# Both FFN matmuls as 2x2 block products with 7 block matmuls instead of 8, weight sums formed on chip, weights streamed once per 1024 tokens

## The chip, the cores and the metric

The kernel runs on all 8 cores of one Trainium2 chip. Each core computes one of the 8 batch elements with the same program and its own copy of the weights in HBM; the cores exchange nothing. The metric is the time on the device, in microseconds, of the slowest core. A core has TensorE (PE, matmuls, with PEld for its weight loads), VectorE (DVE), ScalarE (ACT), GpSimd (POOL) and SyncE (SP), which only issues transfers. POOL issues transfers too, in its own queue, in order with its other instructions.

## The reference

A decoder block on x (2048 tokens by 1024 channels a core). The first part (gated spatial mixing, dilated attention, gates, output projection) is the same in both kernels. The change is in the second part, which is, for each core:

```python
h = rms_norm(x, norm_ffn_pre[l])                       # 2048 x 1024
f = jnp.square(jax.nn.relu(h @ w_ff1[l])) @ w_ff2[l]   # 1024 -> 4096 -> 1024
x = x + rms_norm(f, norm_ffn_post[l])
```

## The kernel before

The program is written as a list of operations with reads, writes and a priority (`P.prio`). A planner (`Plan.schedule`) then plays the list through with a cost for each operation and fixes one static order for each engine's queue; semaphores are put in from the same order. So a change in one place moves instructions in others, and an engine that reaches an instruction whose input isn't there waits, with everything behind it.

The stages in time are: load and norm of x; attention, eight pairs of heads (`hp`), with the value projection for the spatial gating (tiles `hTc`, weights `wva`) mixed into its end; the u projection; gating (`G0`), which for 8 column blocks and 4 token windows runs 32 matmuls each and writes `merged`; output projection for 16 token tiles of 128 (`F0`); FFN (`L0`).

Output projection: for a tile, 16 matmuls into banks 4, 5 or 6, 7; ACT squares them, POOL makes the inverse root, DVE scales (L974), adds x (L976) and scales again (L981), PE transposes the tile and ACT copies it into `h2T`, which shares the memory of `merged`. The first four tiles (`NEARLY`) are done inside the last gating block.

FFN before: four windows `w` of 512 tokens. FFN 1 makes 32 blocks `fb` of 128 hidden channels by 8 matmuls each (128x128 weights, 512 tokens moving), ACT takes relu out of PSUM (L1011), DVE squares (L1012). FFN 2 makes, for each of four token tiles, 2 halves by 32 matmuls; then the norm, the addition of x1 (which was stored to DRAM by the output projection and comes back into `xi[i % 2]`, L1020) and the store of `out` (L1041), both issued by SP. All weights sit in SBUF for the whole FFN: `w1` (8 tiles) and `w2`, bf16. They are f32 in DRAM. Transfers of POOL turn them to bf16 in DRAM during gating (list `conv`, L863 to L869) and load them from there (`load_w1`, `load_w2`), w2 in 16 pieces over the memory of `hT` and `ybT` once FFN 1 has begun.

FFN 1 of window 0 needs only token tiles 0 to 3, so its matmuls stand between those of the output projection of the later tiles.

The softmax here doesn't subtract the row's maximum and nothing guards it: scores larger than these inputs give would overflow.

## Time and profile before

| what | us |
| --- | --- |
| median of 3 runs | 1232.25 (1231.87 to 1414.58) |
| the profiled execution's span | 1230.0 |
| PE busy in it | 1166.0 (95%) |
| DVE busy | 563.4 (46%) |
| ACT busy | 521.4 (42%) |
| DMA engines, share over the FFN | 0.0 to 0.2 |

The span runs from the first to the last instruction of the slowest core and is 2.25 us under the median. Of its stages, attention and everything up to gating end at about 505 us, gating at 725, the output projection at 785, and the last matmul ends at 1222.5. The granted clock of PE is 0.99 of full speed in the mean. The busy shares are of the whole span; what a stage costs is read from its own rows.

### The profile page before, as it was taken

The page shows a single profiled execution, that of the slowest core. Times are in us where ns is not written, and L with a number is a line of the kernel's source. Part 1 is how long each engine was busy: PE and PEld are TensorE (multiplying, and loading weights), DVE is VectorE, ACT ScalarE, POOL GpSimd, SP SyncE. Part 2 cuts the span into 40 slices and gives each one's busy share as a digit, 9 for nine tenths or more (in the row PEclk, how much of TensorE's full clock was granted, in tenths as well). Part 3 has the DMA queues.
Part 4 walks back from the last instruction along what each step waited for, and adds up shares of the span by engine and source line. Part 5 has one row for each costly group of instructions (what it writes and reads, how often), then busy time and mean ns, then how long its engine had stood idle before and what let it go on. Part 6 is the DMA issues. An engine that isn't in the chain of part 4 may idle for free.

```text
span 1230.0 us, 20225 instructions; the slowest of 8 cores (1225.0 to 1230.0 us)
## 1 busy us (share of the span) xinstructions
PE 1166.0 (95%) x7560; PEld 588.8 (48%) x7560; DVE 563.4 (46%) x941; ACT 521.4 (42%) x806; POOL 105.8 (9%) x201
## 2 busy tenths in 40 slices
PE   4799999999898999999999999999999999999997
PEld 2476555665454445444444444444444444444443
DVE  5757777777776346632323357621131122112211
ACT  5437887778765752122121246631132123113311
POOL 0000000001014220000000124410000000000000
PEclk9899999999998999999999999999999999999999
DMA  9464434423313335499968767690200120021011
GB/s 240 126 159 96 115 89 111 106 51 92 80 27 68 63 72 86 84 121 128 128 89 117 120 202 261 226 317 32 76 35 1 65 73 1 3 84 52 1 35 69
DMA packets 59073, 119.91 MB, mean 97 GB/s; under 512 B 36769, under 2 KB 36897, under 8 KB 56482
## 3 DMA queue, kind: packets, MB, share of 16 engines
q0 software_dynamic: 9440, 52.43, 25.7%
q1 hardware_dynamic: 49538, 66.19, 17.5%
q8 instruction: 62, 1.02, 0.3%
q14 instruction: 33, 0.27, 0.1%
HBM read 133.29 MB, written 37.75 MB: 139 GB/s over the span
## 4 chain that ended last, share of the span: by engine, by line
PE 88%; ACT 3%; DVE 3%; issue 3%; DMA 2%; POOL 1%; SPq 0%; ACTq 0%; DVEq 0%; POOLq 0%
PE pst L195 87%; ACT sb_Et L618 2%; DMA sb_xt<-x 1%; PE pst L199 1%; DMA sb_wva<-w_va 1%; DVE sb_xn L489 1%; DVE sb_PT L630 0%; DVE sb_xn L981 0%; POOL sb_st L964 0%; ACT sb_Lr L689 0%; DVE sb_hT L495 0%; ACT sb_junk L966 0%; DVE sb_ybT L694 0%; POOL sb_st L962 0%; ACT sb_gc L798 0%
## 5 line engine op out<-in xcount | busy, mean ns | idle before, releaser
L195 PE MATMUL pst<-sb_w,sb_hid 128*128 128x512 bf16 x1024 | 221.7, 379 | 2.8 <-issue 1.4
L195 PE MATMUL pst<-sb_merged,sb_w 128*128 128x512 bf16 x1024 | 222.8, 379 | 0.0
L618 ACT ACTIVATE sb_Et<-pst 128x1024 bf16<-128x1024 f32 (+1 forms) x160 | 150.4, 973 | 45.5 <-PE pst L195 37.5
L195 PEld LDWEIGHTS pst<-sb_w,sb_hid 128*128 128x128 bf16 x1024 | 100.1, 98 | 124.1 <-issue 3.7
L195 PEld LDWEIGHTS pst<-sb_merged,sb_w 128*128 128x128 bf16 x1024 | 100.1, 98 | 120.1
L1011 ACT ACTIVATE sb_hid<-pst 128x512 bf16<-128x512 f32 x128 | 76.3, 596 | 128.2 <-PE pst L195 127.9
L630 DVE TENSOR_TENSOR sb_PT<-sb_Et,sb_EB 128x1024 bf16<-128x1024 bf16 (+2 forms) x200 | 110.1, 569 | 40.8 <-ACT sb_Et L618 25.6
L195 PE MATMUL pst<-sb_hT,sb_wqk 128*128 128x512 bf16 x512 | 126.4, 394 | 0.9 <-DVE sb_hT L495 0.9
L1012 DVE TENSOR_TENSOR sb_hid<-sb_hid 128x512 bf16<-128x512 bf16 x128 | 54.3, 425 | 142.8 <-ACT sb_hid L1011 141.8
L907 ACT ACTIVATE sb_sg<-pst,sb_small 128x512 f32<-128x512 f32 x64 | 44.0, 687 | 172.7 <-PE pst L195 156.2
L195 PE MATMUL pst<-sb_hT,sb_wg 128*128 128x512 bf16 x512 | 116.7, 379 | 0.0
L1025 ACT ACTIVATE sb_junk<-pst 128x512 bf16<-128x512 f32 x32 | 19.1, 597 | 196.3 <-PE pst L195 196.3
L1028 DVE TENSOR_TENSOR sb_st<-sb_st 128x1 f32<-128x1 f32 x16 | 2.6, 160 | 182.9 <-ACT sb_junk L1025 182.9
L195 PEld LDWEIGHTS pst<-sb_hT,sb_wg 128*128 128x128 bf16 x512 | 49.8, 98 | 58.5
L195 PEld LDWEIGHTS pst<-sb_hT,sb_wqk 128*128 128x128 bf16 x512 | 47.2, 101 | 61.5 <-issue 17.6
L911 DVE SCALAR_TENSOR_TENSOR sb_sg<-sb_sg,pst 128x512 f32<-128x512 f32 x32 | 22.0, 687 | 98.6 <-PE pst L195 98.6
L195 PE MATMUL pst<-sb_wva,sb_hTc 128*128 128x512 bf16 x256 | 61.0, 391 | 4.5 <-DMA sb_wva<-w_va 3.0
L195 PE MATMUL pst<-sb_PT,sb_V 128*128 128x64 bf16 (+3 forms) x1280 | 62.4, 205 | 1.5 <-DVE sb_ybT L694 1.5
L195 PE MATMUL pst<-sb_hT,sb_wu 128*128 128x512 bf16 x256 | 58.9, 387 | 4.7 <-DVE sb_ybT L694 4.1
L195 PE MATMUL pst<-sb_QT,sb_KT 64*128 64x256 bf16 (+1 forms) x768 | 52.7, 250 | 10.7 <-ACT sb_Et L618 10.7
L195 PE MATMUL pst<-sb_ybT,sb_wg 128*128 128x512 bf16 x256 | 60.5, 379 | 1.8 <-DVE sb_tmpm L844 1.8
L195 PE MATMUL pst<-sb_wout,sb_merged 128*128 128x512 bf16 x256 | 58.8, 379 | 1.8 <-DVE sb_xo L972 1.3
(97 smaller groups left out, 1232.7 us busy)
## 6 DMA issues: line engine op xcount, KB each, us to landing
sb_xt<-x SPq DMA_DIRECT2D x16, 512.0 KB, 11.5
sb_xo<-x SPq DMA_DIRECT2D x16, 512.0 KB, 5.8
sb_wg<-w_g POOLq DMA_DIRECT2D x8, 1024.0 KB, 10.8
w_bf<-w POOLq DMA_DIRECT2D x16, 512.0 KB, 10.4
x_scr<-sb_xo SPq DMA_DIRECT2D x16, 512.0 KB, 6.4
sb_xi<-x_scr SPq DMA_DIRECT2D x16, 512.0 KB, 3.7
sb_w<-w_bf POOLq DMA_DIRECT2D x16, 512.0 KB, 17.9
out<-sb_xi SPq DMA_DIRECT2D x16, 512.0 KB, 2.6
```

Of the source, the lines that this page charges most:

```text
L195: e.matmul(out, lhsT=l, rhs=r, start=st, stop=sp, skip_group_check=True))
L199: fns = [lambda e, a=a, b=b: e.transpose(out=a, in_=b, identity=ident) for a, b in outs_ins]
L489: P.dve(lambda e, b=b, n=n, i=i: e.scalar_tensor_tensor(out=xn[n % NXN][:], in0=xt[b][:], scalar=stat[:, 16 + i:17 + i], in1=gbc[:], op0=A ...
L618: P.act(lambda e: e.activation(out=et[:, :, 0:W], in_=psall[:, sb:sb + 2, 0:W], func=AF.Exp, scale=0.125), 2 * W, [], [et.key()], [sb, sb ...
L630: P.dve(lambda e: e.tensor_tensor(out=o, in0=i0, in1=i1, op=ALU.mult), n, rk, [pt.key()], rate=2, name="mask")
L907: P.act(lambda e, j=j, cb=cb, pj=pj, s_=s_: e.activation(out=s_[j][:], in_=pj, func=AF.Tanh, scale=0.5, bias=small[:, bg_c + 8 * j + cb:bg ...
L911: P.dve(lambda e, pj=pj, s_=s_: e.scalar_tensor_tensor(out=s_[1][:], in0=s_[1][:], scalar=1.0, in1=pj, op0=ALU.add, op1=ALU.mult), 512, [s ...
L1011: P.act(lambda e, fb=fb, bk=bk: e.activation(out=hid[:, fb, :], in_=ps(bk), func=AF.Relu), 512, [], [hid.key(fb)], [bk])
L1012: P.dve(lambda e, fb=fb: e.tensor_tensor(out=hid[:, fb, :], in0=hid[:, fb, :], in1=hid[:, fb, :], op=ALU.mult), 512, [hid.key(fb)], [hid.k ...
L1025: P.act(lambda e, hf=hf, bb=bb, s_=s_: e.activation(out=junk4[:, 0:512], in_=ps(bb[hf]), func=AF.Square, accum_out=s_[:, 8 + hf:9 + hf]), ...
L1028: P.dve(lambda e, s_=s_: e.tensor_tensor(out=s_[:, 10:11], in0=s_[:, 8:9], in1=s_[:, 9:10], op=ALU.add), 1, [s_.key((8, 10))], [s_.key((10 ...
```

## The change

FFN 1 and FFN 2 are each written as a product of 2x2 block matrices by 7 block products in place of 8 (sums and differences of blocks of both factors go in, and sums of products come out).

- Weights. Blocks: for FFN 1 the 1024 input channels in 2 halves and the 4096 hidden ones in 2 halves; for FFN 2 the 4096 in 2 and the 1024 in 2. The conversion to bf16 in DRAM is now 32 transfers of POOL, one behind each class of attention (`pv_class`), so that it is done when gating starts. In gating, `prep` (32 times) loads 0.5 MB of four bf16 blocks by SP into a ring `PB`, DVE forms four sums (128x512 each), and SP stores them, 0.5 MB, as `w1_comb` and `w2_comb`.
- Streaming. The FFN runs twice, for `s` = 0, 1, each with 1024 tokens (two windows n1, n2 are the two column blocks). The weights no longer stay in SBUF. A ring of 5 slots takes, by SP, 16 pieces `r1` of 7 blocks (0.92 MB) and 14 pieces `r2` (1.05 MB) in each pass: 58.7 MB in all.
- FFN 1: for each `g` of 16, seven groups (`mmp`) of 4 matmuls into a pair of banks. Between them ACT copies intermediate sums out of PSUM to f32 tiles `sn` (3 a g) and does one relu; DVE adds a PSUM bank and a copy (3 a g, `evict`), does two relus and two squares. DVE forms the token-side sums `TB` and, in place, a quarter of `h2T` ahead of each pass.
- FFN 2: seven block products `o`, each 4 token tiles `p` by 2 halves of hidden channels by 8 matmuls, with DVE forming the sums `S1` and parts of `hid`, copies `s1`, `u2`, `u3` (the same tiles `sn`, 12 in all), and additions `acc`. A token tile is finished (`fin`) behind block product 5 (tiles 4 to 7 of the pass) and 6 (tiles 0 to 3): POOL makes the inverse root; DVE does four operations; the loads of `xi` and the stores of `out` are now issued by POOL. There are still two buffers `xi`.
- Matmuls of both FFN parts: 1792 in place of 2048, each 128x128 by 512 as before.

```diff
+    conv = []
+    for g in range(16):
+        conv.append(lambda g=g: P.dma("pool", lambda e: e.dma_start(out=w1b_d[g], in_=w1_d[g]), 1e6, f"cv{g % 2}", [],
+                                      [P.nkey(("w1b", g))], after=anchor[0]))
+    for h in range(4):
+        for q in range(4):
+            c = slice(2048 * h, 2048 * h + 2048)
+            conv.append(lambda q=q, h=h, c=c: P.dma("pool", lambda e: e.dma_start(out=w2b_d[q][:, c], in_=w2_d[q][:, c]), 1e6, f"cv{q % 2}", [],
...
+            if conv:
+                P.prio = b0 + (11 + 3 * c) * 5 + 1
+                conv.pop(0)()
...
+    def prep(n, prio):
+
+        g = n % 16
+        pb = PB[n % 4 if n < 24 else n % 2]
+        ki, ko = pb.key((0, 4)), pb.key((4, 8))
+        c = f"pb{n % 4 if n < 24 else n % 2}"
+        if n < 16:
+            P.dma("sp", lambda e: e.dma_start(out=pb[:, 0:4, :].rearrange("p q c -> p (q c)"), in_=w1b_d[g]), 0.5e6, c + "l",
+                  [P.nkey(("w1b", g))], [ki], prio=prio)
+        else:
+            P.dma("sp", lambda e: e.dma_start(out=pb[:, 0:4, :], in_=w2b_d.rearrange("q p c -> p q c")[:, :, 512 * g:512 * g + 512]), 0.5e6,
+                  c + "l", [P.nkey(("w2b", q, g // 4)) for q in range(4)], [ki], prio=prio)
+        for o, i0, i1, op in ((4, 0, 3, ALU.add), (5, 4, 1, ALU.subtract), (6, 1, 0, ALU.subtract), (7, 2, 5, ALU.subtract)) if n < 16 else (
+                (4, 0, 1, ALU.subtract), (5, 3, 4, ALU.subtract), (6, 3, 0, ALU.subtract), (7, 2, 5, ALU.subtract)):
+            P.dve(lambda e, o=o, i0=i0, i1=i1, op=op: e.tensor_tensor(out=pb[:, o, :], in0=pb[:, i0, :], in1=pb[:, i1, :], op=op), 512,
+                  [pb.key(i0), pb.key(i1)], [pb.key(o)], prio=prio + 3, rate=2, name="comb")
+        if n < 16:
+            P.dma("sp", lambda e: e.dma_start(out=w1c_d[g], in_=pb[:, 4:8, :].rearrange("p q c -> p (q c)")), 0.5e6, c + "s", [ko],
+                  [P.nkey(("w1c", g))], prio=prio + 4)
+        else:
+            P.dma("sp", lambda e: e.dma_start(out=w2c_d.rearrange("q p c -> p q c")[:, :, 512 * g:512 * g + 512], in_=pb[:, 4:8, :]), 0.5e6,
+                  c + "s", [ko], [P.nkey(("w2c", g))], prio=prio + 4)
     rot = [0]
...
-        if 2 <= cb < 4:
-            load_w1(cb - 2, G0 + 20 * cb)
...
-            if conv and it >= 4:
-                P.prio = G0 + 20 * cb + 5 * w + 2
-                conv.pop(0)()
...
+            prep(it, G0 + 20 * cb + 5 * w - (6 if it else 0))
...
+    hid = buf("hid", 0, [16, 2, 1024])
+    TB = buf("TB", 96 * K, [3, 4, 512])
+    S1 = buf("S1", 108 * K, [16, 512])
...
+    NRING = 5
+    RO = [152, 160, 168, 192, 184]
...
+    SNO = [144, 146, 148, 150, 128, 130, 132, 134, 136, 138, 140, 142]
+    sn = [buf(f"sn{i}", o * K, [512], F32) for i, o in enumerate(SNO)]
...
+        p = LS - 5
+        tt(TB[:, 0], h2T[:, 0:4, n2], h2T[:, 0:4, n1], ALU.subtract, [h2T.key(lo, k1), h2T.key(lo, k2)], TB.key(0), p)
+        tt(TB[:, 1], h2T[:, 4:8, n2], TB[:, 0], ALU.subtract, [h2T.key(hi, k2), TB.key(0)], TB.key(1), p)
+        tt(h2T[:, 0:4, n2], h2T[:, 4:8, n2], h2T[:, 0:4, n2], ALU.subtract, [h2T.key(hi, k2), h2T.key(lo, k2)], h2T.key(lo, k2), p)
+        tt(TB[:, 2], h2T[:, 4:8, n1], TB[:, 1], ALU.subtract, [h2T.key(hi, k1), TB.key(1)], TB.key(2), p)
...
+            P.dma("sp", lambda e, g=g, wt=wt: e.dma_start(out=wt[:, 0:3].rearrange("p q k c -> p (q k c)"), in_=w1b_d[g][:, 512:2048]), 0.4e6,
+                  f"rg{rs}a", [P.nkey(("w1b", g))], [wt.key((0, 3))], prio=tp0 - 60)
+            P.dma("sp", lambda e, g=g, wt=wt: e.dma_start(out=wt[:, 3:7].rearrange("p q k c -> p (q k c)"), in_=w1c_d[g]), 0.5e6,
+                  f"rg{rs}b", [P.nkey(("w1c", g))], [wt.key((3, 7))], prio=tp0 - 59.9)
+            bs = bset[0] % 4
+            bset[0] += 1
+            ba, bb_ = 2 * bs, 2 * bs + 1
+            s1, u2, u3 = [sn[(3 * (g % 4) + j)] for j in range(3)]
...
+            mmp(0, 0, "B11", ba, True)
+            snap(s1, ba)
+            mmp(1, 1, "B21", bb_, True)
+            evict(0, 0, s1, bb_)
+            mmp(2, 4, "T2", ba, False)
+            snap(u2, ba)
+            mmp(3, 3, "T1", bb_, True)
+            mmp(4, 5, "T3", ba, False)
+            snap(u3, ba)
+            evict(1, 1, u3, bb_)
+            relu(1, 512, 1024)
+            mmp(5, 2, "T4", ba, False)
+            P.act(lambda e, g=g, ba=ba: e.activation(out=hid[:, g, 1, 0:512], in_=ps(ba), func=AF.Relu), 512, [], [hid.key(g, 1, (0, 512))], [ba])
+            square(1, 0, 1024)
+            mmp(6, 6, "B22", bb_, False)
+            evict(0, 1, u2, bb_)
+            relu(0, 0, 1024)
+            square(0, 0, 1024)
...
+        s1, u2, u3 = sn[0:4], sn[4:8], sn[8:12]
+        st_ = {}
+        for o, (nm, src, q, bank0, start) in enumerate((("A11", "b", 1, 0, True), ("A12", "b", 2, 4, True), ("S", "c", 0, 4, True),
+                                                        ("S", "c", 1, 0, False), ("S3", "c", 2, 0, False), ("A22", "c", 3, 0, False),
...
+                if o == 2:
+                    tt(S1[:, gs, c], S1[:, gs, c], hid[:, gs, 0, c], ALU.subtract, [S1.key(gk, kc), hid.key(gk, 0, kc)], S1.key(gk, kc), P.prio + 3, 1024)
+                if o == 3:
+                    tt(hid[:, gs, 1, c], hid[:, gs, 1, c], S1[:, gs, c], ALU.subtract, [S1.key(gk, kc), hid.key(gk, 1, kc)], hid.key(gk, 1, kc),
+                       P.prio + 20, 1024)
...
+                def fin(i, halves, c0, sp_=sp_):
+                    x_ = xi[i % 2]
+                    kx = x_.key()
+                    P.dma("pool", lambda e: e.dma_start(out=x_[:], in_=x1_d[i]), 512e3, f"xi{i % 2}", [P.nkey(("x1", i))], [kx], prio=P.prio - 12)
+                    P.pool(lambda e: e.tensor_tensor(out=sp_[:, c0 + 2:c0 + 3], in0=sp_[:, c0:c0 + 1], in1=sp_[:, c0 + 1:c0 + 2], op=ALU.add), 0.25,
+                           [sp_.key((c0, c0 + 2))], [sp_.key((c0 + 2, c0 + 3))])
+                    P.pool(lambda e: e.tensor_scalar(out=sp_[:, c0 + 2:c0 + 3], in0=sp_[:, c0 + 2:c0 + 3], scalar1=1.0 / DM, scalar2=EPS,
+                                                     op0=ALU.mult, op1=ALU.add), 0.25, [sp_.key((c0 + 2, c0 + 3))], [sp_.key((c0 + 2, c0 + 3))])
+                    P.pool(lambda e: e.tensor_tensor(out=sp_[:, c0 + 3:c0 + 4], in0=sp_[:, c0 + 2:c0 + 3], in1=nhalf[:, 0:1], op=ALU.pow), 0.6,
+                           [sp_.key((c0 + 2, c0 + 3)), nhalf.key()], [sp_.key((c0 + 3, c0 + 4))])
...
+                    for hf, (src, k, bks) in enumerate(halves):
+                        hs = slice(512 * hf, 512 * hf + 512)
+                        P.dve(lambda e, src=src, hs=hs: e.scalar_tensor_tensor(out=src, in0=src, scalar=sp_[:, c0 + 3:c0 + 4], in1=gfin[:, hs],
+                                                                              op0=ALU.mult, op1=ALU.mult), 512, [rk, gfin.key()] + k, k, bks)
+                        P.dve(lambda e, src=src, hs=hs, x_=x_: e.tensor_tensor(out=x_[:, hs], in0=src, in1=x_[:, hs], op=ALU.add), 512,
+                              [kx] + k, [x_.key((512 * hf, 512 * hf + 512))], bks)
+                    P.dma("pool", lambda e, i=i, x_=x_: e.dma_start(out=toks(out_d, i), in_=x_[:]), 512e3, f"xs{i % 2}", [kx], [])
+                if o == 0:
+                    snp(s1[p])
+                elif o == 1:
+                    acc(s1[p], bk)
+                    sq(s1[p][:], 8, [s1[p].key()], [])
+                elif o == 3:
+                    snp(u2[p])
+                elif o == 4:
+                    snp(u3[p])
+                    acc(u3[p], 4 + p)
+                    sq(u3[p][:], 13, [u3[p].key()], [])
+                elif o == 5:
+                    sq(ps(bk), 12, [], [bk])
+                    fin(8 * s + 4 + p, [(ps(bk), [], [bk]), (u3[p][:], [u3[p].key()], [])], 12)
+                elif o == 6:
+                    acc(u2[p], bk)
+                    sq(u2[p][:], 9, [u2[p].key()], [])
+                    fin(8 * s + p, [(s1[p][:], [s1[p].key()], []), (u2[p][:], [u2[p].key()], [])], 8)
     P.schedule()
...
```

How the static orders of the engines move, at three places. A row is the line in the program, the operation, the tiles with the planner's buffer number, and in brackets the semaphores it waits for.

PE in the output projection, from the first FFN 1 group between its tiles on, in the kernel before (`sb_w_0` is the first of the eight tiles of w1, `sb_xn` the tile that is transposed):

```order
L195 MATMUL pst<-sb_merged,sb_w_0_156 128x512 [waits s_act,d_w1_0]
L195 MATMUL pst<-sb_merged,sb_w_0_156 128x512 x7
L195 MATMUL pst<-sb_wout,sb_merged 128x512 [waits s_dve]
L195 MATMUL pst<-sb_wout,sb_merged 128x512 x7
L199 MATMUL pst<-sb_ident,sb_xn_0_173 128x128 [waits s_dve]
L199 MATMUL pst<-sb_ident,sb_xn_0_173 128x128 x7
L195 MATMUL pst<-sb_wout,sb_merged 128x512 x8
L199 MATMUL pst<-sb_ident,sb_xn_1_174 128x128 [waits s_dve,s_act]
L199 MATMUL pst<-sb_ident,sb_xn_1_174 128x128 x7
L195 MATMUL pst<-sb_wout,sb_merged 128x512 x16
L195 MATMUL pst<-sb_merged,sb_w_0_156 128x512 x8
```

The same place in the changed kernel (`sb_r_0` is the ring's first slot):

```order
L195 MATMUL pst<-sb_merged,sb_r_0_187 128x512 [waits s_act,d_rg0a]
L195 MATMUL pst<-sb_merged,sb_r_0_187 128x512 x3
L195 MATMUL pst<-sb_wout,sb_merged 128x512 [waits s_dve]
L195 MATMUL pst<-sb_wout,sb_merged 128x512 x7
L199 MATMUL pst<-sb_ident,sb_xn_0_167 128x128 [waits s_dve]
L199 MATMUL pst<-sb_ident,sb_xn_0_167 128x128 x7
L195 MATMUL pst<-sb_wout,sb_merged 128x512 x8
L195 MATMUL pst<-sb_wout,sb_merged 128x512 [waits s_dve]
L195 MATMUL pst<-sb_wout,sb_merged 128x512 x7
L199 MATMUL pst<-sb_ident,sb_xn_1_168 128x128 [waits s_dve,s_act]
L199 MATMUL pst<-sb_ident,sb_xn_1_168 128x128 x7
L195 MATMUL pst<-sb_wout,sb_merged 128x512 x8
L195 MATMUL pst<-sb_merged,sb_r_0_187 128x512 x4
```

The FFN 1 groups between the tiles now have 4 matmuls where they had 8.

SP at the end of the kernel before, with the loads and stores of the two buffers `xi` (`x1_scr` holds x1; `d_xs0` is the landing of the last store out of buffer 0):

```order
L1020 DMA sb_xi0_190<-x1_scr 128x1024 [waits d_xs0]
L1041 DMA out<-sb_xi1_191 128x1024 [waits s_dve]
L1020 DMA sb_xi1_191<-x1_scr 128x1024 [waits d_xs1]
L1041 DMA out<-sb_xi0_190 128x1024 [waits s_dve]
L1041 DMA out<-sb_xi1_191 128x1024 [waits s_dve]
```

POOL at the end of the changed kernel (`sb_st2`, `sb_st3` are the statistics of token tiles 2 and 3 of a pass):

```order
L1165 TENSOR_TENSOR sb_st2_180<-sb_st2_180,sb_nhalf_182 128x1 [waits s_pool]
L1161 TENSOR_TENSOR sb_st3_181<-sb_st3_181 128x1 [waits s_act]
L1160 DMA sb_xi0_209<-x1_scr 128x1024 [waits d_xs0]
L1163 TENSOR_SCALAR sb_st3_181<-sb_st3_181 128x1 [waits s_pool]
L1165 TENSOR_TENSOR sb_st3_181<-sb_st3_181,sb_nhalf_182 128x1 [waits s_pool]
L1160 DMA sb_xi1_210<-x1_scr 128x1024 [waits d_xs1]
L1174 DMA out<-sb_xi0_209 128x1024 [waits s_dve]
L1174 DMA out<-sb_xi1_210 128x1024 [waits s_dve]
L1160 DMA sb_xi0_209<-x1_scr 128x1024 [waits d_xs0]
L1160 DMA sb_xi1_210<-x1_scr 128x1024 [waits d_xs1]
L1174 DMA out<-sb_xi0_209 128x1024 [waits s_dve]
L1174 DMA out<-sb_xi1_210 128x1024 [waits s_dve]
```

The loads and stores of `xi` have moved from SP's queue into POOL's, two and two, with the statistics of the last tiles among them.

POOL late in attention, around the last piece of the weights `wva`, in the kernel before:

```order
L767 COPY sb_hTc_128<-sb_hT 128x1024 [waits s_pe]
L767 COPY sb_hTc_129<-sb_hT 128x1024
L767 COPY sb_hTc_130<-sb_hT 128x1024 [waits s_pe]
L742 DMA sb_wva<-w_va 128x2048 [waits s_pe]
L767 COPY sb_hTc_133<-sb_hT 128x1024 [waits s_dve]
```

And now (`w_bf` is a conversion of FFN weights; `d_cv0`, `d_cv1` are the landings of the two before it):

```order
L781 COPY sb_hTc_129<-sb_hT 128x1024
L583 DMA w_bf<-w 128x2048 [waits s_pe,d_cv0]
L781 COPY sb_hTc_130<-sb_hT 128x1024
L583 DMA w_bf<-w 128x2048 [waits s_pe,d_cv1]
L756 DMA sb_wva<-w_va 128x2048 [waits s_pe]
L583 DMA w_bf<-w 128x2048 [waits s_pe,d_cv0]
L583 DMA w_bf<-w 128x2048 [waits s_pe,d_cv1]
L583 DMA w_bf<-w 128x2048 [waits s_pe,d_cv0]
L781 COPY sb_hTc_133<-sb_hT 128x1024 [waits s_dve]
```

Conversions now stand ahead of and behind that load, between the copies `hTc`.

## Rows read from the trace of the kernel before

**Rows 1.** The page: span and busy shares of the engines.

```profile
span 1230.0 us, 20225 instructions; the slowest of 8 cores (1225.0 to 1230.0 us)
...
PE 1166.0 (95%) x7560; PEld 588.8 (48%) x7560; DVE 563.4 (46%) x941; ACT 521.4 (42%) x806; POOL 105.8 (9%) x201
```

**Rows 2.** Windows: busy us (xcount) of each engine, then PEclk, DMA share, GB/s.

```profile
core 6: us, PE busy (x) PEld busy (x) DVE busy (x) ACT busy (x) POOL busy (x), PEclk, DMA share, GB/s
725.11:784.85 59.74, 55.95 (x323) 27.17 (x321) 44.23 (x40) 38.61 (x63) 23.04 (x48) 1.00 0.73 242
785.00:834.25 49.25, 49.25 (x241) 22.57 (x238) 16.50 (x32) 21.34 (x36) 12.59 (x25) 1.00 0.90 288
...
1166.99:1222.46 55.47, 55.41 (x256) 24.95 (x256) 8.57 (x15) 6.04 (x20) 0.00 (x0) 1.00 0.13 48
1222.46:1230.00 7.54, 0.00 (x0) 0.00 (x0) 2.86 (x5) 1.09 (x4) 0.00 (x0) 0.73 0.17 70
```

**Rows 3.** Groups by shape: busy us, mean ns of one, idle before and its releaser.

```profile
L195 PE MATMUL pst<-sb_merged,sb_w 128*128 128x512 bf16 x1024 | 222.8, 379 | 0.0
L195 PE MATMUL pst<-sb_w,sb_hid 128*128 128x512 bf16 x1024 | 221.7, 379 | 2.8 <-issue 1.4 <-DVE sb_hid L1012 1.4
...
L630 DVE TENSOR_TENSOR sb_PT<-sb_Et,sb_EB 128x1024 bf16<-128x1024 bf16 x120 | 83.2, 709 | 26.4 <-ACT sb_Et L618 12.8 <-PE pst L195 12.1
...
L535 DVE COPY sb_KT<-sb_KT 128x512 bf16<-128x512 bf16 x32 | 23.2, 738 | 0.7
...
L1039 DVE TENSOR_TENSOR sb_xi<-pst,sb_xi 128x512 f32<-128x512 f32 x32 | 21.9, 686 | 1.4
...
L981 DVE SCALAR_TENSOR_TENSOR sb_xn<-sb_xo,sb_st,sb_gpre 128x1024 bf16<-128x1024 f32 x16 | 20.5, 1280 | 4.7 <-POOL sb_st L964 4.7
...
L974 DVE SCALAR_TENSOR_TENSOR sb_tp<-pst,sb_st,sb_gpost 128x1024 f32<-128x1024 f32 x12 | 15.4, 1284 | 12.5 <-POOL sb_st L964 12.5
L976 DVE TENSOR_TENSOR sb_xo<-sb_tp,sb_xo 128x1024 f32<-128x1024 f32 x12 | 14.7, 1223 | 1.2 <-DVE sb_tp L974 1.2
```

**Rows 4.** Timeline of TensorE, two transposes that waited: start, us, operation, idle before.

```profile
743.89 0.61 PE L199 MATMUL pst<-sb_ident,sb_xn 128*128 128x128 bf16 x8 [0.69 <-DVE sb_xn L981]
...
754.37 0.61 PE L199 MATMUL pst<-sb_ident,sb_xn 128*128 128x128 bf16 x8 [0.80 <-DVE sb_xn L981]
```

**Rows 5.** Timeline of TensorE at two stalls late in attention: start, us.

```profile
327.66 3.10 PE L195 MATMUL pst<-sb_wva,sb_hTc 128*128 128x512 bf16 x8 [2.97 <-DMA sb_wva<-w_va]
...
383.74 3.57 PE L195 MATMUL pst<-sb_hT,sb_wu 128*128 128x512 bf16 x8 [4.08 <-DVE sb_ybT L694]
387.11 4.86 PE L195 MATMUL pst<-sb_wva,sb_hTc 128*128 128x512 bf16 x16
```

**Rows 6.** Transfers: queue, count, KB each, median us from issue to landing.

```profile
sb_xo<-x SPq DMA_DIRECT2D x16, 512.0 KB, 5.8
...
w_bf<-w POOLq DMA_DIRECT2D x16, 512.0 KB, 10.4
...
out<-sb_xi SPq DMA_DIRECT2D x16, 512.0 KB, 2.6
...
sb_wu<-w_u POOLq DMA_DIRECT2D x8, 256.0 KB, 5.5
```

**Rows 7.** Landing min, median, max: the tile xi (loads and stores), then wva.

```profile
DMA to landing us min/median/max: 2.6/3.3/8.7
...
DMA to landing us min/median/max: 5.9/6.7/8.7
```

**Rows 8.** Windows again: attention, two of weight conversion, one of the w2 load.

```profile
180.00:200.00 20.00, 20.00 (x254) 15.19 (x251) 13.04 (x21) 13.38 (x17) 1.25 (x2) 1.00 0.39 66
...
520.00:540.00 20.00, 20.00 (x95) 9.07 (x93) 6.21 (x9) 3.87 (x6) 1.54 (x3) 1.00 1.12 145
560.00:580.00 20.00, 20.00 (x94) 9.11 (x93) 6.20 (x9) 3.59 (x6) 1.07 (x2) 1.00 0.93 108
...
800.00:820.00 20.00, 20.00 (x94) 9.11 (x93) 5.11 (x12) 6.98 (x12) 5.40 (x10) 1.00 0.99 300
```

175 lines of the change are left out of this document (103 added, 72 removed).

## The prediction, made before the changed kernel had run

> **What bounds the kernel now.** I read the page first, then stretches of windows, then the groups by shape, then the timeline at the few places where PE waits. The span is 1230.0 us and PE is busy 1166.0 of it [rows 1]. In the FFN it is busy throughout: the last stretch has 256 matmuls in 55.47 us, 0.2158 us each, at granted clock 1.00, with DVE at 8.6 us and DMA at 0.13 [rows 2]. Both FFN groups have 1024 matmuls, and all that PE lost at them is 2.8 us [rows 3]. So the FFN is bound by the number of matmuls, and the other engines and the DMA have room. The output projection is different: 59.74 us with PE idle 3.8 and DVE busy 44.2 [rows 2], its transposes waiting 0.7 to 0.8 us for DVE every second tile, 10.5 us apart [rows 4]. Behind the last matmul come 7.5 us [rows 2].
>
> The profiled execution spans 1230.0 us, the median is 1232.25; I work in the span and add 2.25.
>
> **What goes away.** 2048 - 1792 = 256 matmuls at 0.2158 us are 55.2 us [rows 2]. The two gaps of 1.4 us [rows 3] were FFN 1 to FFN 2 turns (the load of w2; the last square): the new order starts FFN 2 with the block whose inputs are oldest, so I take them off too: 58.0 us in all.
>
> **Attention, +5 (0 to 12).** The conversions move here, 32 transfers of POOL, one about every 9.5 us. Two windows of conversion show 108 to 145 GB/s at a share of 0.93 to 1.12; one such transfer lands in 10.4 us [rows 6, 8]. Attention's share is 0.39 [rows 8]; a conversion of 0.5 MB at about 125 GB/s is 4 us of all engines, so the share goes to about 0.8. The loads of V are issued some 40 us ahead and stay hidden. One load isn't: PE already waits 2.97 us for the last piece of `wva` [rows 5], which lands in up to 8.7 us [rows 7], and two conversions now stand ahead of it in POOL's queue. I add half a conversion's 4 us, with the clock: behind each of the two stalls the next matmuls ran at the lower level, 3.10 and 3.57 us where 8 take 1.89 [rows 5]. With about 1.5 for that and as much for POOL's copies `hTc`, also behind conversions, I take 5. Nothing if POOL's queue has drained; 12 if a whole landing is added.
>
> **Gating, 0 (to +2).** `prep` adds 128 DVE operations of 128x512 bf16. By the 128x1024 row (0.709 us) they are at most 0.43 each [rows 3], 1.7 us in a window of 6.9, where DVE has 6.2 us of work in 20 [rows 8]. That makes 55%. The cover is the second set of four banks: a `prep` that lands up to some 5 us late costs nothing, and 0.5 MB land in 5.8 us [rows 6]; without it each late landing would stop PE for its excess.
>
> **Output projection, +6.5 (3 to 11).** FFN 1 groups filled PE here: five of 8 matmuls, 8.6 us. Now only sums of tokens 0 to 7 release most of them, and six groups of 4 stand there, 5.2 us: 3.4 us less filling. DVE gets four operations `TB` of 2048 elements (twice the 0.709 row less its start, 1.3 each) and some `evict` (0.69) [rows 3], 7 us more on top of 12 tiles at 1.28 + 1.22 + 1.28 = 3.8 us, so 45 + 7 = 52 of 60 us, with its waits for POOL unchanged. I let 3 of the 7 lengthen the stage. None if they fit its idle time, which leaves the 3.4; 7.5 if all of it does, which makes 11.
>
> **FFN 1 in its steady part, 0 (to +2).** A `g` costs PE 28 x 0.2158 = 6.04 us. DVE: three `evict` at 0.69, two squares at 0.71, `S1` and `hid` sums 2 x 1.3 every fourth `g`, 0.65 [rows 3]: 4.1, and relu on 512 and 1024. No row shows a bf16 tensor_scalar in SBUF; the nearest, a strided copy, has 512 in 0.74 [rows 3], which bounds both from above at 2.1; from below I take a third, 0.7. Four operations that wait for their forerunner add about 0.1 each. So 5.2 to 6.6; I take 5.4, under 6.04: PE covers it, and up to 2 us go to waits as `S1` comes by. The Trainium skill, VectorE: DVE Perf Modes, "The perf-mode tier table", gives tensor_scalar the 4x rate on bf16 in SBUF (693 ns for 2048); by that the two are about 0.7 us. No row here shows it.
>
> **Streaming, 0.** 58.7 MB over 1792 x 0.2158 = 387 us are 152 GB/s. The w2 load ran at 300 GB/s with all cores doing the same [rows 8]. Four slots ahead of the one in use are 24 us of matmuls.
>
> **The end, +14.7 (7 to 27).** This is the term I chose most in. There are two `xi` buffers, and block products 5 and 6 finish eight token tiles within 19 us; before, a tile came every 13.8 us. So a buffer goes: two additions (0.69 each), store, load, two additions. The store lands in 2.6 us and the tile's transfers in 3.3 on SP [rows 6, 7]; now POOL issues them. The nearest POOL rows: 256 KB land in 5.5 us median [rows 6]. I take 3.1 for a store and 4.2 for a load, nearer to SP's since the queues are empty there. With 1.4 for additions and 0.7 for handoffs a round is 9.4 us. Let T be the end of block product 5. The first pair of tiles is stored by about T + 4.7 (the first three tiles' statistics and the DVE work of one and a half, 0.69 to 0.76 an operation). Three rounds and a store: T + 4.7 + 28.2 + 3.1 = T + 36. The last matmul ends at T + 13.8 (64 x 0.2158). The tail is 22.2 us where it is 7.5 now [rows 2]: +14.7. Bounds: store and load both 2.6, the lowest of rows 7: rounds of 7.0, +7; both 5.5: rounds of 12.8, +27. The Trainium skill, DMA: Bandwidth & Descriptors, "Anatomy of one DMA — SWDGE (gpsimd) path", has 2.0 us + bytes/436e3, 3.2 us for 512 KB; by that the estimate for rounds is 8.5 and for the end +12.
>
> **Between the passes, +11 (2 to 17).** The same chain runs with the ring loading beside it; I take rounds of 11.4 (a load as `xo` lands, 5.8 [rows 6]). FFN 1 of the second pass can't have its tiles `sn` until `fin` has added them: the last pair's first tile is added at T + 1.7 + 3 x 11.4 = T + 36. Until then PE has block product 6 (13.8 us) and 16 groups of 4 (13.8 us), to T + 27.6, and small waits within a single `g` of about 2 us, which fall in the same time. So PE loses 36 - 27.6 = 8 us, and by the clock 3 more: after 4.08 us idle it lost 1.7 and then 1.2 us [rows 5]. That is 11. With rounds of 7 all is covered but the small waits, 2; with 12.8 it is 14 + 3 = 17. DVE's queue adds: `evict` stands behind additions that wait for `xi`.
>
> **Sum.** 1230.0 - 58.0 + 5 + 6.5 + 14.7 + 11 = 1209.2, + 2.25: 1211 us. All lower ends: 1230 - 58 + 3 + 7 + 2 + 2.25 = 1186. All upper: 1230 - 58 + 12 + 2 + 11 + 2 + 27 + 17 + 2.25 = 1245.
>
> **Rivals.**
> - *The chain is short* (transfers land as fast from POOL as from SP, and POOL isn't late). End +9, between passes +3, attention and projection 3 each: 1192 us. For it: 2.6 and 3.3 us [rows 6, 7]. Against: the POOL rows. 0.27.
> - *The chain is long* (5.5 us a transfer): end +23, between +17, attention and projection 8 each: 1230 us, almost no gain. For it: the POOL rows, and POOL's queue, where a load waits for the landing of a store ahead of it, and the statistics of later tiles stand ahead of loads. Against: those rows are conversions of twice the bytes in. 0.13.
> - *DVE becomes the bound in FFN 1*: with the relus at the copy row's rate a `g` takes DVE 6.6 us or more; over 32 `g` up to 0.86 each, 27 us: 1238. 0.05.
> - *The ring starves* (the one on the other side): if 58.7 MB move at the 145 to 108 GB/s of the conversion windows [rows 8], the FFN takes 405 to 543 us in place of 387. It decides below 152 GB/s, and the kernel is over 2% slower below 136 (433 us): 1257 and more, 1300 in the middle. Against: those are casts from DRAM to DRAM; 300 GB/s stands for loads. 0.05.
> - *The forecast*, 0.50, with its own range 1202 to 1221.
>
> **Chances.** A measurement of this kernel tells 2% from no change: 1207.6 and 1256.9 us. Faster: the short chain, 0.27, and a quarter of the forecast's case, 0.12: 0.39. Slower: 0.05. Same: 0.56. The range takes the short and most of the long case: 1190 to 1236.
>
> **What would show it.** In the new profile: 1792 FFN matmuls at 0.216 us; between the last matmul and the end 15 to 35 us with loads and stores of `xi` in turns, DVE waiting for DMA; the same turns between the passes with a PE gap of 5 to 10 us and a lower PEclk behind it; DVE at 85 to 90% in FFN 1 with PE at 1.00; no PE wait for `sb_r`. A first `wva` wait near 6 us. It is wrong if the `xi` chain is under 7 us a round, if PE waits for DVE or `sb_r` within FFN 1, or if attention's slots move by more than 12 us.

## The result, and the profile after

The changed kernel takes 1243.2 us (median) where the kernel before takes 1231.9: a ratio of 1.008, interval 1.0063 to 1.0097. So it is slower by 0.8%, though it has 256 matmuls less. Some executions ran in a slower state (two of five of the changed kernel, one of five of the kernel before): the medians here are over all of them, while the ratios leave those out. The forecast was 1211, the range 1190 to 1236. The profiled execution spans 1237.7 us, against 1230.0 [rows 1].

The page of the changed kernel: span, busy time of the engines, and from the 40 slices the granted clock and the DMA share; last, the DMA share of the kernel before.

```profile
span 1237.7 us, 20810 instructions; the slowest of 8 cores (1227.1 to 1237.7 us)
PE 1120.9 (91%) x7304; PEld 565.4 (46%) x7304; DVE 740.3 (60%) x1229; ACT 529.3 (43%) x797; POOL 139.8 (11%) x267
PEclk9899999999899999999999999999999988999995
DMA  9467878878747557589962228474454475454424
...
DMA  9464434423313335499968767690200120021011
```

PE is busy 45 us less than before, and the span is 7.7 us longer: 53 us more in which PE does nothing. The slices say where: a lower clock from about 990 to 1050 us (8 in two slices), a last slice with hardly any matmul in it, and a DMA share of mostly 7 or 8 tenths through attention where it was mostly 3 or 4.

The place where each stage begins, from the timeline of PE, before first, then after: the first group of gating that reads `yaT`, and a group of 24 matmuls of the output projection that stands behind the same wait (1.3 us) in both.

```profile
505.62 5.34 PE L195 MATMUL pst<-sb_yaT,sb_wg 128*128 128x512 bf16 x24
730.05 5.34 PE L195 MATMUL pst<-sb_wout,sb_merged 128*128 128x512 bf16 x24 [1.32 <-DVE sb_xo L972]
...
521.05 5.34 PE L195 MATMUL pst<-sb_yaT,sb_wg 128*128 128x512 bf16 x24
752.29 5.34 PE L195 MATMUL pst<-sb_wout,sb_merged 128*128 128x512 bf16 x24 [1.31 <-DVE sb_xo L985]
```

Gating starts 15.4 us later, and takes 231.2 us in place of 224.4: 6.8 more. From the second mark to the last matmul it is 454.1 us (to 1206.4) in place of 492.4. Less 58.0 would be 434.4, so 19.7 are lost there. Behind the last matmul come 31.3 us where there were 7.6. The four sum up: -58.0 + 15.4 + 6.8 + 19.7 + 23.7 = +7.6.

These are the stages of the slowest core, and which core that is matters. Before, the eight cores start gating between 500.5 and 505.6 us; changed, between 511.0 and 521.1. In the median of the cores gating starts 11.3 us later, takes 6.4 more, 19.1 are lost from the second mark to the last matmul, and the tail is 24.5 longer. So some 4 of the 15.4 us before gating are the wider spread of the cores, not what a typical core loses.

**Before gating.** What PE waited for between 290 and 520 us (engine, line, releaser: us in total, times, longest), the largest rows:

```profile
PE pst L195 <- DMA sb_wva<-w_va: 8.6, 1, 8.6
PE pst L195 <- ACT sb_Et L629: 5.4, 9, 1.9
PE pst L195 <- DVE sb_BS L824: 4.1, 1, 4.1
PE pst L195 <- DVE sb_tmpm L858: 3.6, 2, 1.9
PE pst L195 <- POOL sb_hTc L781: 3.2, 1, 3.2
PE pst L195 <- DVE sb_bst L805: 1.8, 1, 1.8
```

The wait for `wva` was 2.97 us [rows 5] and is 8.6. Those for `BS` and `bst` are new; `hTc` stands in the place of the old wait of 4.08 [rows 5]. Behind the two new ones are waits for transfers: DVE stood 4.9 us in front of `BS` until `b_s` had landed, and 3.7 us in front of `wsTf` until `wsT` had. From issue to landing, `wva` took up to 16.7 us (8.7 before [rows 7]), and `b_s` 17.5 us (4.6 before). Conversions of POOL are issued on both sides of `wva`, at 297, 306, 315 and 326 us, and four more from 371 to 389, beside `b_s`.

**Gating.** What DVE waited for at the sums of weights in the whole program (the view as above), then the timeline around the one long wait of PE in gating, DVE and PE:

```profile
DVE sb_PB L889 <- DMA sb_PB<-w_bf: 45.0, 14, 8.5
...
617.96 0.42 DVE L889 TENSOR_TENSOR sb_PB<-sb_PB 128x512 bf16<-128x512 bf16 x1 [4.91 <-DMA sb_PB<-w_bf]
618.30 0.69 DVE L933 TENSOR_TENSOR sb_merged<-sb_mA,sb_sg 128x512 bf16<-128x512 f32 x1
...
627.86 1.10 DVE L889 TENSOR_TENSOR sb_PB<-sb_PB 128x512 bf16<-128x512 bf16 x3 [7.87 <-DMA sb_PB<-w_bf]
628.88 0.68 DVE L927 SCALAR_TENSOR_TENSOR sb_sg<-sb_sg,pst 128x512 f32<-128x512 f32 x1
...
629.70 2.75 PE L195 MATMUL pst<-sb_ybT,sb_wg 128*128 128x512 bf16 x7 [4.89 <-DVE sb_sg L927]
```

A sum of weights stands in DVE's queue; its load isn't there; the gating operation behind it (L927) has had its inputs for long, and PE needs the bank that it frees. Most of DVE's waits cost PE nothing: 12 of the 14 lie in gating, 43.7 us in all, with single ones of 7.9 and 8.5 us (to 573.6 and 600.5 us) during which PE went on at full work. PE stopped once, 4.9 us, where a wait of 7.9 came 10 us behind one of 4.9. The rest of the 6.8 us is the clock: the next two groups of 8 matmuls took 3.2 and 2.3 us in place of 1.9. From 540 to 600 us the DMA share is 0.97 to 1.03.

**Between the passes.** Windows of 20 us (from:to, us, busy time and count of PE, PEld, DVE, ACT, POOL, then granted clock, DMA share, GB/s), PE's timeline at the two longest waits, and the waits of ACT and DVE behind them (whole program):

```profile
980.00:1000.00 20.00, 19.21 (x90) 8.55 (x89) 13.34 (x22) 3.58 (x10) 9.35 (x20) 1.00 0.72 213
1000.00:1020.00 20.00, 12.06 (x42) 4.17 (x40) 9.44 (x16) 3.48 (x6) 4.94 (x10) 0.81 0.70 244
1020.00:1040.00 20.00, 16.30 (x63) 6.89 (x64) 12.74 (x23) 6.71 (x12) 2.35 (x4) 0.76 0.63 210
...
1010.74 1.87 PE L195 MATMUL pst<-sb_merged,sb_r 128*128 128x512 bf16 x4 [2.75 <-DVE sb_hid L1067]
1023.70 1.87 PE L195 MATMUL pst<-sb_TB,sb_r 128*128 128x512 bf16 x4 [6.84 <-ACT sb_sn L1064]
...
ACT sb_sn L1064 <- DVE sb_xi L1172: 11.2, 2, 8.0
DVE sb_xi L1172 <- DMA sb_xi<-x_scr: 19.9, 5, 5.8
```

195 matmuls where three full windows have 279: 84 x 0.2158 = 18.1 us lost. The waits in it sum to 12.3 us; the other 5.8 I put down to the clock. ACT's copy into `sn` waits for `fin` to have read that tile, and `fin` for `xi`. Of the 19.7 us, 1.6 are left for all the rest: output projection, DVE in FFN 1, streaming.

**The end.** POOL's timeline behind the last matmul (1206.4), from the first full round; and the last piece of the chain that ended last:

```profile
1215.26 0.54 POOL L1174 DMA_DIRECT2D out<-sb_xi  x1 [3.17 <-DVE sb_xi L1172]
1218.47 0.54 POOL L1174 DMA_DIRECT2D out<-sb_xi  x1 [2.68 <-DMA out<-sb_xi]
1219.00 0.55 POOL L1160 DMA_DIRECT2D sb_xi<-x_scr  x1
1221.95 0.55 POOL L1160 DMA_DIRECT2D sb_xi<-x_scr  x1 [2.40 <-DMA out<-sb_xi]
1225.79 0.54 POOL L1174 DMA_DIRECT2D out<-sb_xi  x1 [3.30 <-DVE sb_xi L1172]
1228.64 0.54 POOL L1174 DMA_DIRECT2D out<-sb_xi  x1 [2.31 <-DVE sb_xi L1172]
...
1228.62 0.56 POOLq L337
```

A round is 10.2 to 10.5 us (1215.26 to 1225.79, 1218.47 to 1228.64). The last store is issued at 1228.64 and lands in 2.9 us, at 1231.5. The span ends at 1237.7, 6.1 us later. The view gives 0.56 us for the last piece, at line 337, where the block of the program ends; the trace's record of that instruction, a DRAIN on POOL, runs for 8.80 us, from 1228.62 to 1237.42, and every other engine waits for it. All eight cores end 9.0 us behind the issue of their last store; before, with SP, it was 2.9 (1227.08 to 1230.0).

**FFN itself.** From 820 to 900 us PE has 94 or 95 matmuls in each 20 us at clock 1.00, and DVE is busy 63.9 of 80 us. The page has 640 + 512 + 384 matmuls in its rows and the groups have 256 more (`sb_r,sb_S`): 1792. PE never waits for a load of `sb_r`. The share of 0.0 to 0.2 given ahead for the FFN of the kernel before holds behind its load of `w2`; up to about 834 us it was 0.9 [rows 2].

### The profile page after: what moved, and what is told of

It is laid out like the page before. It is cut to its first block, busy times and chain, and to the rows that moved or that the text cites. A ratio compares the mean times of both kernels' runs of the same rounds, so it can differ in the third digit from the quotient of the medians.

```text
span 1237.7 us, 20810 instructions; the slowest of 8 cores (1227.1 to 1237.7 us)
## 1 busy us (share of the span) xinstructions
PE 1120.9 (91%) x7304; PEld 565.4 (46%) x7304; DVE 740.3 (60%) x1229; ACT 529.3 (43%) x797; POOL 139.8 (11%) x267
## 4 chain that ended last, share of the span: by engine, by line
PE 70%; DMA 13%; DVE 6%; issue 4%; ACT 4%; POOL 2%; SPq 0%; DVEq 0%; POOLq 0%; ACTq 0%
PE pst L195 70%; DMA sb_PB<-w_bf 6%; ACT sb_Et L629 2%; DMA sb_xi<-x_scr 2%; DMA sb_BS<-b_s 1%; DMA out<-sb_xi 1%; DMA sb_wva<-w_va 1%; DMA sb_xt<-x 1%; DVE sb_PB L889 1%; PE pst L199 1%; DVE sb_xi L1172 1%; ACT sb_Lr L700 0%; DVE sb_xn L491 0%; ACT sb_junk L484 0%; POOL sb_st L1165 0%
## 5 line engine op out<-in xcount | busy, mean ns | idle before, releaser
L195 PE MATMUL pst<-sb_r,sb_hid 128*128 128x512 bf16 x640 | 139.1, 379 | 0.0
L195 PE MATMUL pst<-sb_merged,sb_r 128*128 128x512 bf16 x512 | 123.0, 383 | 3.5 <-DVE sb_hid L1067 2.8
L195 PE MATMUL pst<-sb_TB,sb_r 128*128 128x512 bf16 x384 | 96.9, 390 | 8.9 <-ACT sb_sn L1064 7.7
L1064 ACT ACTIVATE sb_sn<-pst 128x512 f32<-128x512 f32 x96 | 57.1, 597 | 111.1 <-PE pst L195 99.7
L195 PEld LDWEIGHTS pst<-sb_r,sb_hid 128*128 128x128 bf16 x640 | 62.6, 98 | 75.6
L195 PEld LDWEIGHTS pst<-sb_merged,sb_r 128*128 128x128 bf16 x512 | 50.1, 99 | 64.9 <-issue 7.6
L889 DVE TENSOR_TENSOR sb_PB<-sb_PB 128x512 bf16<-128x512 bf16 x128 | 49.1, 419 | 46.4 <-DMA sb_PB<-w_bf 45.0
L1067 DVE TENSOR_TENSOR sb_hid<-pst,sb_sn 128x512 bf16<-128x512 f32 x96 | 65.2, 687 | 14.8 <-PE pst L195 10.1
L1151 DVE TENSOR_TENSOR sb_sn<-pst,sb_sn 128x512 f32<-128x512 f32 x24 | 16.5, 689 | 88.4 <-ACT sb_sn L1148 50.2
L195 PEld LDWEIGHTS pst<-sb_TB,sb_r 128*128 128x128 bf16 x384 | 38.2, 100 | 57.4 <-issue 15.6
L195 PE MATMUL pst<-sb_QT,sb_KT 64*128 64x256 bf16 (+1 forms) x768 | 52.3, 248 | 12.5 <-ACT sb_Et L629 12.5
## 6 DMA issues: line engine op xcount, KB each, us to landing
sb_xt<-x SPq DMA_DIRECT2D x16, 512.0 KB, 12.6
```

The lines of the kernel that those rows point to most:

```text
L195: e.matmul(out, lhsT=l, rhs=r, start=st, stop=sp, skip_group_check=True))
L889: P.dve(lambda e, o=o, i0=i0, i1=i1, op=op: e.tensor_tensor(out=pb[:, o, :], in0=pb[:, i0, :], in1=pb[:, i1, :], op=op), 512, [pb.key(i0), ...
L1064: P.act(lambda e: e.activation(out=o[:], in_=ps(bk), func=AF.Copy), 512, [], [o.key()], [bk], name="snap")
L1067: P.dve(lambda e, g=g: e.tensor_tensor(out=hid[:, g, h, 512 * nn:512 * nn + 512], in0=ps(bk), in1=a[:], op=ALU.add), 512, [a.key()], [hid. ...
L1151: P.dve(lambda e: e.tensor_tensor(out=d[:], in0=ps(bk), in1=d[:], op=ALU.add), 512, [d.key()], [d.key()], [bk])
```

## The experiments

Four prices were to be told apart: landings stretched by conversions (before gating), sums that stand too early in DVE's queue (gating), the chain through two `xi` buffers (between the passes and at the end), and what POOL's queue does at the very end. The table gives each run's median and its ratio to executions of the kernel before made beside it (their medians go from 1231 to 1233 us, so the ratios are the sharper comparison), with times of its slowest core: start of gating (the first mark above), gating (to the second mark), from there to the last matmul, and the tail.

| kernel | median | ratio (interval) | gating starts | gating | to last matmul | tail |
| --- | --- | --- | --- | --- | --- | --- |
| before | 1231.9 | | 505.6 | 224.4 | 492.4 | 7.6 |
| changed | 1243.2 | 1.008 (1.0063 to 1.0097) | 521.0 | 231.2 | 454.1 | 31.3 |
| e1: 7 `xi` | 1215.1 | 0.985 (0.9819 to 0.9882) | 518.1 | 237.5 | 437.7 | 20.1 |
| e2: `xi`, `out` on SP | 1228.8 | 0.9944 (0.9923 to 0.9965) | 519.0 | 236.5 | 451.6 | 20.1 |
| e3: both | 1204.4 | 0.9768 (0.975 to 0.9785) | 517.3 | 234.1 | 439.4 | 11.3 |
| e4: no combinations | 1230.3 | 0.9993 (0.9983 to 1.0004) | 521.2 | 225.3 | 455.9 | 29.6 |
| e5: 9 conversions | 1229.4 | 0.9967 (0.995 to 0.9984) | 508.9 | 234.0 | 454.9 | 29.5 |
| e6: e3, sums spaced | 1194.8 | 0.9703 (0.9682 to 0.9725) | 521.7 | 225.5 | 435.7 | 12.5 |
| e7: e3, 8 conversions late | 1219.3 | 0.9903 (0.9884 to 0.9923) | 535.5 | 233.5 | 436.0 | 12.2 |
| e8: e6 and e7 | 1192.6 | 0.9685 (0.9664 to 0.9705) | 515.0 | 227.1 | 435.8 | 12.8 |
| e9: e8, 12 late | 1192.4 | 0.9681 (0.9667 to 0.9695) | 516.6 | 225.9 | 436.0 | 12.6 |
| e10: before, `out` on POOL | 1238.2 | 1.0057 (1.0041 to 1.0073) | 505.4 | 224.8 | 492.3 | 14.0 |
| e11: e9, queues spaced | 1204.5 | 0.9782 (0.9768 to 0.9796) | 525.3 | 225.7 | 437.6 | 12.3 |
| e12: e11, 3 early sums | 1198.7 | 0.9756 (0.9733 to 0.9779) | 523.7 | 224.7 | 436.4 | 12.4 |

Among the eight cores of one run the start of gating differs by 4 to 14 us, and gating itself by up to 12 where DVE waits in it, so a difference of a few us in these two columns needs the other cores beside it. The last two columns differ by up to 6 us in the changed kernels with two `xi` buffers and by about 2 in the others.

### The chain and POOL's end: e1, e2, e3, e10

e1, seven buffers (block product 5 comes after the last reader of `S1`):

```diff
-    xi = [buf(f"xi{i}", (176 + 4 * i) * K, [1024], F32) for i in range(2)]
+    xi = [buf(f"xi{i}", o * K, [1024], F32) for i, o in enumerate((176, 180, 200, 108, 112, 116, 120))]
...
-                    x_ = xi[i % 2]
+                    xn_ = (i % 8 + 4) % 8 % 7
+                    x_ = xi[xn_]
...
```

> The changed kernel with seven buffers xi in place of two (three in the free places beside the ring, four in S1, which nobody reads any more when the first tile is finished); loads and stores stay on POOL. Theory 1 (the chain store, load, add through two buffers sets the end and the gap between the passes): every load lands long before its tile, so the tail from the last matmul to the end falls from 31.3 to about 16 us (additions and square 1.5, statistics 1.8, four DVE operations 2.9, handoffs 1, store 2.9, and 6.1 that POOL needs behind its last store), and the 18 us that PE loses between the passes fall to 2 to 4: median 1243 - 30 = 1213 us. Theory 2 (the amount of finishing work on DVE, ACT and POOL sets both): tail 25 us or more, loss between the passes over 12, median 1230 or more.

1215.1 us. From the second mark to the last matmul it is 437.7 us in place of 454.1. The same three windows as above, now of e1:

```profile
980.00:1000.00 20.00, 20.00 (x94) 9.06 (x93) 15.06 (x24) 4.83 (x13) 12.01 (x28) 1.00 0.76 228
1000.00:1020.00 20.00, 18.66 (x86) 8.01 (x85) 17.05 (x30) 7.83 (x15) 4.54 (x9) 1.00 0.89 305
1020.00:1040.00 20.00, 20.00 (x94) 9.05 (x93) 15.33 (x25) 8.13 (x14) 0.00 (x0) 1.00 0.50 178
```

274 matmuls, clock 1.00: 5 missing, 1.1 us. The amount of finishing work is the same and DVE is busier in these windows than before, so theory 2 falls: the buffers were the price. The tail is 20.1, not 16: the last store is issued 11.1 us behind the last matmul (I had 7). The statistics of two tiles pass POOL one after the other there, behind a store that waits for DVE.

e2, the queue alone:

```diff
-                    P.dma("pool", lambda e: e.dma_start(out=x_[:], in_=x1_d[i]), 512e3, f"xi{i % 2}", [P.nkey(("x1", i))], [kx], prio=P.prio - 12)
+                    P.dma("sp", lambda e: e.dma_start(out=x_[:], in_=x1_d[i]), 512e3, f"xi{i % 2}", [P.nkey(("x1", i))], [kx], prio=P.prio - 12)
...
-                    P.dma("pool", lambda e, i=i, x_=x_: e.dma_start(out=toks(out_d, i), in_=x_[:]), 512e3, f"xs{i % 2}", [kx], [])
+                    P.dma("sp", lambda e, i=i, x_=x_: e.dma_start(out=toks(out_d, i), in_=x_[:]), 512e3, f"xs{i % 2}", [kx], [])
```

> The changed kernel with the loads of xi and the stores of out issued by SP, as in the kernel before; still two buffers. In the trace of the changed kernel the last store lands 2.9 us after its issue, but the span goes on for 6.1 us. Theory 1 (this is the price of a POOL store at the very end, and the chain of rounds stays): tail 31.3 - 6.1 - 1 to 3 for shorter landings = 22 to 24 us, between the passes still 14 to 18 us lost, median 1232 to 1236. Rival (the 6.1 us have nothing to do with POOL's queue): tail 28 to 30, median 1239 to 1242.

The tail is 20.1 us: 11.2 less, not the 7 to 9 expected. About 6 are POOL's end. The rest are shorter rounds, 9.6 and 8.0 us: SP's pairs of stores start at 1204.33, 1213.89 and 1221.91. Most of the loss between the passes stays (451.6 us to the last matmul, 454.1 with POOL). 1228.8, below the 1232 to 1236 expected.

e3 has both edits.

> Both edits: seven buffers, transfers on SP. Theory (chain and POOL's closing wait are two separate prices that add): tail about 10 us, 2 to 4 us lost between the passes, median about 1207. If SP's queue, which also loads the ring, holds back weights behind a store that waits for DVE, PE shows waits for sb_r and the median stays at 1213 or above.

1204.4 us, tail 11.3; no operation waited for `xi`, and SP's queue never held back a weight. The tail falls by 8.8 against e1: the last store is issued 8.0 us behind the last matmul in place of 11.1, and the end comes 3.4 us behind its issue in place of 9.0. So about 3 are the order in POOL's queue and nearly 6 its end.

e10 asks for that price in the other kernel, where there is no chain and no ring:

```diff
-            P.dma("sp", lambda e, i=i, x_=x_: e.dma_start(out=toks(out_d, i), in_=x_[:]), 512e3, f"xs{i % 2}", [kx], [])
+            P.dma("pool", lambda e, i=i, x_=x_: e.dma_start(out=toks(out_d, i), in_=x_[:]), 512e3, f"xs{i % 2}", [kx], [])
```

> The kernel before with one edit: the 16 stores to out are issued by POOL in place of SP. PE's order is the same. Theory (a POOL store at the very end costs about 6 us behind its landing): span +6 to +7, median 1237.5 to 1239. Rival (the 6.1 us seen in the changed kernel come from its chain of loads and stores, not from the queue): within 1 us of the kernel before.

1238.2 us. The last issue and its landing, of e10:

```profile
1227.67 0.53 POOL L1041 DMA_DIRECT2D out<-sb_xi  x1 [13.28 <-DVE sb_xi L1039]
...
out<-sb_xi POOLq DMA_DIRECT2D x1, 512.0 KB, 2.9
```

It has landed at 1230.6, and the span is 1236.5: 5.9 us behind the landing. The last matmul ends where it did (1222.5). So the price belongs to POOL's queue at the end of the program, not to the chain. The DRAIN at line 337 runs 8.63 us on POOL here, from the issue on.

Is it the store that POOL's end waits for? Mostly not. In e3 POOL issued its last transfer at 676 us, and still its DRAIN took 6.5 us behind its last instruction (1194.2 to 1200.8 us, and the same length on all eight cores); it was over before SP's last store had landed at 1201.5, so it cost nothing. What costs is that POOL is the last engine to finish.

### Gating: e4, e6

e4 takes the combinations out:

```diff
-            prep(it, G0 + 20 * cb + 5 * w - (6 if it else 0))
...
-                srcd = w2b_d if src == "b" else w2c_d
+                srcd = w2b_d
...
```

and loads `w1b_d[g]` where `w1c_d[g]` was.

> The changed kernel without its 32 weight combinations: no loads into PB, no DVE sums, no stores of combinations; the ring reads plain converted weights of the same size in their place, so what the FFN computes is not the block product. Theory (DVE stands in front of a late PB load, gating's own DVE work waits behind it, and PE behind that): the 4.9 us wait in gating and the slower clock behind it go, 6 to 10 us: median 1233 to 1237. Rival (the combinations also cost elsewhere, by their share of the DMA engines before gating): 1229 or less. Third: no gain (1243), if the wait only moves to another load such as gating's own weights.

Gating takes 225.3 us, 5.9 less, nearly all of the loss there; on all eight cores it takes 224.4 to 225.3, where the changed kernel has 227.3 to 235.7. The start of gating doesn't move (521.2), so the combinations cost nothing before it. The span falls by 5.7 (1237.7 to 1232.0); the ratio falls by 0.9%, 10.7 us, above the theory's 6 to 10 and near the rival's number, though not for the rival's reason. The other 5 us are mostly a matter of which executions were profiled: the changed kernel's was its shortest (1239.2 us, median 1243.2), e4's lay 3.2 us above its median (1233.5 and 1230.3).

e6 keeps every byte and every sum, moves them, and lets the first five share one buffer of `PB`:

```diff
+    for n in range(5):
+        prep(n, G0 - 6 + n, 2)
+    pit = {n: n - 4 if n < 28 else (25, 26, 28, 29)[n - 28] for n in range(5, 32)}
...
-            prep(it, G0 + 20 * cb + 5 * w - (6 if it else 0))
+            for n, i_ in pit.items():
+                if i_ == it - 1:
+                    prep(n, G0 + 5 * it - 3, 1, gp[it, 2 if n < 26 else 3])
+            for n, i_ in pit.items():
+                if i_ == it:
+                    prep(n, G0 + 5 * it, 0, gp[it, 0])
```

`prep` is split into its load (part 0) and its sums and store (part 1), each released by a matmul group `gp[step, j]` of gating.

> Seven xi buffers on SP (1204.4 us), and the 32 combinations kept but spaced: 5 before gating, then one for each step of gating, its load released by a matmul group of the step and its DVE sums by a group of the next step, about 12 us behind the load. Same bytes, same sums. Theory (what costs in gating is where the sums stand in DVE's order, not that they exist): PE has no wait in gating, 7 to 10 us less: 1195 to 1197 us. Rival (the bytes themselves cost): no gain, 1204.

1194.8 us against e3's 1204.4, and 8 us less by the ratios. Gating takes 225.5 us where e3 has 234.1 (over the cores 224.7 to 226.9 and 227.0 to 234.1), and what PE waits for in it is 0.4 us. So bytes and sums can be hidden, and the rival is out: what cost up to 9 us was when they came. The edit changes two things at once, though. The sums stand later behind their loads, and the loads are spread out: in e6 the DMA share from 540 to 600 us is 0.62 to 0.77, and a load of `PB` lands in 6.3 us in the median of gating where e3 has 10.2. No run has one without the other.

Behind the second mark e6 also needs 3.7 us less than e3 (435.7 for 439.4). There e3 has two windows of 20 us (980 to 1020) at clock 0.94 and 0.93 though PE is busy 19.9 us in each, and e6 has 1.00; no run says why.

### Before gating: e5, e7, e8, e9, e11, e12

e5 has 9 conversions in place of 32, and all readers use those:

```diff
-    for g in range(16):
+    for g in range(1):
...
-    for h in range(4):
+    for h in range(2):
         for q in range(4):
...
```

> The changed kernel with 9 of the 32 conversions (one block of W1, half of W2), and every later reader of converted weights pointed at these: the same loads and sums everywhere behind, but of the wrong weights. The 23 conversions from 180 us on are gone, those that run while wva, the gate weights' transpose and b_s are loaded. Theory (conversions stretch the landings of others: wva 16.7 us where it was 8.7, wsT 11.9 for 4.4, b_s 17.5 for 4.6): of the 15.4 us by which gating starts later, 12 to 15 go: median 1228 to 1231. If something else in the change delays these stages, the median stays within 4 us of 1243.

Gating starts at 508.9: 12.1 of the 15.4 us are gone (in the median of the cores 9.1 of 11.3). PE's waits from 290 to 530 us in e5, the same view as above:

```profile
PE pst L195 <- DVE sb_ybT L705: 5.6, 3, 4.1
PE pst L195 <- DVE sb_tmpm L858: 3.6, 2, 1.9
PE pst L195 <- ACT sb_gv L797: 2.8, 3, 1.6
PE pst L195 <- ACT sb_Et L629: 2.8, 6, 0.6
PE pst L195 <- DMA sb_wva<-w_va: 1.5, 1, 1.5
```

1229.4 us, as the theory has it: `wva` 1.5 for 8.6, no `BS`, no `hTc`; `b_s` lands in 4.8 us. Shown: the conversions do it. Whether by their place in POOL's queue or by their share of the DMA engines, this run doesn't separate.

e7 keeps them all, and moves the last eight behind attention:

```diff
-            if conv:
+            if conv and hp < 6:
...
-        anchor[0] = P.ops[-1]
+        anchor[0] = P.ops[-2]
+        P.prio = U0 + 10 * g + 6
+        conv.pop(0)()
```

> Seven xi buffers on SP (1204.4 us), and the last 8 of the 32 conversions moved from the last quarter of attention to the stage of u behind it, one per 12 us. Theory (these conversions stretch the landings of wva, wsT and b_s): waits at wva back to about 3 us and none at b_s; gating starts 8 to 12 us earlier: 1193 to 1197 us. Rival (conversions cost wherever they stand, since the stage of u has DVE and POOL work too): 1204.

1219.3: worse than e3 by 15 us, a miss of both forecasts. The new wait, from PE's timeline, and DVE's waits from 405 to 530 us, of e7:

```profile
507.04 1.24 PE L195 MATMUL pst<-sb_wsT,sb_gc 128*128 128x128 bf16 x8 [16.11 <-DVE sb_tmpm L860]
...
DVE sb_PB L891 <- DMA sb_PB<-w_bf: 24.9, 4, 19.9
```

The wait for `BS` is gone, but a combination waits 19.9 us for its load, with the operation that PE needs behind it: the fault of gating in another place. The DMA share is 1.01 from 460 to 500 us, with the conversions beside those loads. The wait for `wva` stays at 6.4, since attention still has conversions at 289, 298, 306 and 316 us.

e8 has both e6 and e7.

> Both of these edits on the seven buffers with SP. If the two prices are separate they add: 1204.4 - 8 - 9 = 1187 us, 3.7% below the kernel before. If the late conversions meet the combinations (both want the DMA engines from 405 to 600 us), less than the better of the two alone: 1195 or more.

1192.6: neither forecast, and 2 us under e6, which the intervals of the two don't tell apart (0.9664 to 0.9705 and 0.9682 to 0.9725). With the sums spaced, the conversions in the stage of u cost no more than they save.

e9 takes the four conversions from 288 us on out of attention too; the last five now stand in gating.

```diff
-            if conv:
+            if conv and hp < 5:
...
+        if g:
+            conv.pop(0)()
...
+            if conv:
+                P.prio = G0 + 5 * it + 3
+                anchor[0] = gp[it, 0]
+                conv.pop(0)()
...
```

> Like e8_both, but attention keeps only 20 conversions, so none stands in the queue around the last piece of wva (those at 288, 297, 306 and 315 us are gone); 7 stand in the stage of u and 5 in the first steps of gating, each released by a matmul group further back, so that POOL doesn't wait in front of the statistics behind it. Theory (wva's landing is stretched by the conversions just ahead of it in the same queue): the wait at wva falls from 5.1 to between 1 and 3 us, the waits for gv and yaT (4.9 and 4.0 in e8) by half: 1183 to 1187 us. If the landing of wva is stretched only by the loads of V beside it: wait still 5, 1190 to 1193 us.

1192.4: the rival's number, not for the rival's reason. `wva` behaves as the theory says: PE waits 0.8 to 2.3 us for it on seven cores, and the first `wva` matmul of the slowest core is at 328.7 us (327.7 before). But that core gets it back in waits for `gv` (7.2 us), `hTc` (4.5) and `Lr` (3.0). The cores part: 1176.2 to 1191.2 us, and the slowest one is the time. Core 3, at 1176.2, starts gating at 502.9 us, where the cores of the kernel before start it from 500.5 to 505.6: it shows what is there when little is late.

e11 spaces the early sums by matmul groups of u (`up[g]`) and gives the conversions four semaphores for two.

```diff
-        prep(n, G0 - 6 + n, 2)
+        prep(n, U0 + 10 * (n + 2), 0, up[n + 1])
+        prep(n, U0 + 10 * (n + 3), 1, up[n + 2])
...
```

> Like e9_all, with the queues behind attention made to wait less: the five combinations ahead of gating have their loads and sums released by matmul groups of the stage of u (a sum about 12 us behind its load, as in gating), and conversions take turns on four semaphores in place of two, so that one doesn't wait in POOL's queue for the landing of the one before. In e9 DVE stood 5.25 us in front of such a sum at 441 us, POOL 3.96 us in front of a conversion at 432 us, and PE waited 7.2 us for gv behind them. Theory (what e9 lost in the stage of u is order in DVE's and POOL's queues): these waits go, gating starts 5 to 8 us earlier, 1184 to 1188 us. Rival (the stage is limited by transfers or by the cores' own spread): 1190 to 1193 us.

1204.5, a miss of theory and rival. PE's waits from 395 to 530 us, then DVE's, of e11:

```profile
PE pst L195 <- DVE sb_tmpm L863: 20.0, 5, 9.0
PE pst L195 <- ACT sb_gv L797: 0.8, 1, 0.8
...
DVE sb_PB L899 <- DMA w_comb<-sb_PB: 24.6, 2, 14.1
```

The waits for `gv` are gone (0.8), and the last `wva` matmul is at 442.5, earlier than before (446.7). The five sums share one buffer, though, and two of them now wait for the store of the one ahead (up to 19.7 us to its landing).

e12 has three early combinations, with a matmul group two blocks of u further on for each.

```diff
-    for n in range(5):
+    for n in range(3):
-        prep(n, U0 + 10 * (n + 2), 0, up[n + 1])
-        prep(n, U0 + 10 * (n + 3), 1, up[n + 2])
+        prep(n, U0 + 20 * (n + 1), 0, up[2 * n + 1])
+        prep(n, U0 + 20 * (n + 1) + 10, 1, up[2 * n + 2])
...
```

> Like e11_order, but with three combinations in the stage of u in place of five, each with twice the time, and 29 in gating. In e11 the five shared one buffer PB: a round (load, sums, store of up to 19.7 us to its landing) didn't fit 12 us, so DVE stood 24.6 us in front of sums whose outputs were still being stored, and PE waited 20.0 us for tmpm behind them, while the waits for gv were gone (0.8 us). Theory (only that buffer's turnaround was left): no wait of DVE for a store there, PE's waits for tmpm back to 2.6 us, gating starts near 508 us: 1183 to 1188 us. Rival (DVE meets the same waits at the new places in gating, with more combinations there): 1190 to 1195 us.

1198.7: DVE now waits 22.5 us for two loads, the longest 14.0, and PE 14.1 for `tmpm`. The rival is nearer, and the time lies above its range too. A load or store of `PB` takes up to 16.9 us to land, more than the places that e11 and e12 gave the early sums allow. That stage wasn't settled: 9 to 11 us of the 15.4 remain in the best kernels, e8 and e9.

## Why the prediction was wrong, point by point

| term | on record | range | measured | from |
| --- | --- | --- | --- | --- |
| matmuls and the two turns | -58.0 | | -58.0; with the rows marked * together -56.4 | marks |
| attention, up to gating | +5 | 0 to 12 | +15.4 | marks |
| gating | 0 | to +2 | +6.8 | marks |
| output projection * | +6.5 | 3 to 11 | at most +1.6 | the rest |
| FFN 1, DVE * | 0 | to +2 | about 0 | no PE wait 820 to 900 us |
| streaming * | 0 | | 0 | no wait for `sb_r` |
| between the passes | +11 | 2 to 17 | +18.1 | 84 matmuls |
| the end | +14.7 | 7 to 27 | +23.7 | 31.3 - 7.6 |

The sum was 28 us short: 10.4 + 6.8 + 7.1 + 9.0, less 4.9. The other 3 us are the step from span to median, 5.5 us here for the 2.25 taken. Two steps failed in their mechanism, attention and gating: loads that were held to be hidden or in time weren't. Two terms had the right mechanism and the wrong size: the gap between the passes and the end. Attention's term is above even its own upper bound, and the prediction's sign for that (a move of more than 12 us) came. That the time lies within 2% of the kernel before, which had been given 0.56, is luck: a sum that was to bring 1.7% lost 0.8%.

- **What goes away: right.** 1792 matmuls at 0.2158 us. In e6, where the long waits are gone, PE needs 435.7 us where 434.4 are the sum's.
- **Attention: the step that failed** is "The loads of V are issued some 40 us ahead and stay hidden. One load isn't". I looked for loads that PE already waited for, and found one. I didn't look at those with little slack: `wsT` and `b_s` landed in 4.4 and 4.6 us before and were first used 9.7 and 13.3 us behind their issue. With conversions beside them they took 11.9 and 17.5. For `wva` I added half a conversion's share of the engines, 2 us; its landing doubled, 8.7 to 16.7. The share I gave (0.8) is what the windows show (0.74 and 0.82).
- **Gating: the step that failed** is "a `prep` that lands up to some 5 us late costs nothing, and 0.5 MB land in 5.8 us". The landing failed: 9.9 us in the median from 590 to 640 us, where the planner puts 95 of the 128 sums between 516 and 633 us, with nothing to space them. The cover was no worse than said: single waits of DVE up to 8.5 us cost PE nothing, but I had one late load in mind and not two in a row. I spread 32 evenly over gating; the static order doesn't.
- **Output projection: over-priced**, 1.6 at most for 6.5. That groups of 4 stand there in place of 8, and the added DVE work, together cost no more than that.
- **FFN 1: right.** DVE is busy 80% (85 to 90 foretold), the relus take 0.43 us for 1024 elements and 0.29 for 512, 0.72 a `g` (0.7 foretold), and the rival that DVE becomes the bound is dead. The two rows (294 and 427 ns) give an estimate of 427 + 2 x (427 - 294) = 693 ns for 2048 elements, a size that no run has. The Trainium skill, VectorE: DVE Perf Modes, "The perf-mode tier table", states 693 ns for `tensor_scalar` on 2048 bf16 elements in SBUF. The estimate from this trace agrees.
- **Between the passes: right in kind, 18.1 for 11.** The mechanism was the one foretold and e1 shows it. Waits were 12.3 us for the 8 of the sum, and the clock 5.8 for 3. The rounds were mis-sized: stores of a buffer stand 16.1, 14.3 and 12.4 us apart where I had 11.4, and PE was let go some 43 us behind the end of block product 5 where I had 36. PE ran in pieces of one to six groups between waits, with the clock at 0.81 and 0.76 in two windows.
- **The end: right in kind, 23.7 for 14.7.** T is 1192.6; the last landing comes at T + 38.9 for T + 36, with rounds of 10.7 in the mean (11.0, 11.1 and 10.2) for 9.4. The other 6.1 are POOL's end, which no row of the kernel before showed: its last instruction is SP's. I set the price of the change of queue at the transfer's landing alone. The Trainium skill, DMA: Bandwidth & Descriptors, "Anatomy of one DMA — SWDGE (gpsimd) path", gives a fit by which such a transfer takes 3.2 us, an estimate. In this trace the stores at the end took 2.9 us and the loads of the last rounds some 4.5.

Some of the prediction's own working doesn't come out of its terms: rounds with both transfers at 2.6 or 5.5 us are 7.3 and 13.1, not 7.0 and 12.8, a load of 5.8 makes rounds of 11.0, not 11.4, and rounds of 12.8 leave a gap of 12.5 us between the passes, not 14. For DVE as the bound, 6.6 us a `g` exceeds 6.04 by 0.56, which is 18 us, not 27. Each of them is under 2 us but the last, and none moves the forecast by more than 1 us.

Of the rivals, the long chain (1230) was nearest in kind. Between the passes its rounds came, and longer ones; at the end its 5.5 us a transfer didn't (2.9 and 4.5). The ring never starved: in four windows from 820 to 900 us 126 to 207 GB/s moved with PE at full work.

All in all the gain of 58 us was there. It was given back in four places. In three an engine stood in order in front of a landing; the fourth, the end, was that and POOL's own closing. The chain of `xi` and POOL's end were bought back, 39 us in all, by memory that lay free and by a change of queue (e3). The best kernels, e8 and e9, are 3.2% under the kernel before.

## What to carry to other kernels

Before an edit adds transfers to a stretch, list every load there that is used within some three times its landing, not only those that PE waits for now (here `b_s` was used 13.3 us behind its issue with a landing of 4.6), and price each at two to four times its landing: the three here took 1.9, 2.7 and 3.8 times as long as before. In a static order, an operation that waits for a transfer should be released by work that ends well after the landing is due; where this planner had no such release it placed it early, and what stood behind it paid. And count a double buffer by its round (store, load, compute): when the work that uses it comes in a burst, two are too few. Here seven buffers for a burst of eight tiles took the loss between the passes away; numbers between two and seven weren't tried.

## What the runs showed of the hardware that was not expected

The end of these programs costs 6 us more if POOL has issued the last store: the landing is 2.9 us behind the issue, and the span goes on to 9.0 (changed kernel, all eight cores) or 8.8 (e10), where with SP it ends 0.3 us (before, e2) to 1.0 us (e6) behind the landing. In e10 that is a ratio of 1.0057, 7.0 us, for one word of source. The time is one DRAIN on POOL. Its length goes with the number of transfers that POOL has issued in the whole program: 8.80 us for 100 (changed kernel), 8.63 for 98 (e10), 6.92 for 77 (e5, which ends 7.1 us behind its last store), and 6.55 for 68 (e2, e3 and all the kernels built on e3), where the last of them lay over 450 us back and the DRAIN was hidden behind SP's stores. The kernel before is apart: its POOL finishes at 816 us right behind its loads of `w2`, and that DRAIN took 17 to 21 us. No run changes that number and nothing else, and that a program which ends on a POOL instruction without a transfer pays the 6.5 us wasn't tried. Here it pays to let POOL finish well ahead of the last store.

Also, cores that run the same program part. They parted by 5.0 us in the kernel before, by 10.6 in the changed one, by 15.0 in e9 (1176.2 to 1191.2) and by 18.1 in e5, but by 7.0 in e8, and the slowest one is the time. In e5 it is one place: gating takes 225.5 us on three cores and 233 to 234 on five. Why a given core meets a late landing and another doesn't, these runs don't show.
